# Hybrid attention and recurrence trunk: GpSimd's order waits taken out, its block products moved, and the recurrence's normalisation moved from ScalarE to VectorE

## The reference

```python
od = diff_attention(q, k, v, lam)         # 4 heads, two softmax maps each, block-causal mask of 64-token chunks
    # w = softmax(q1 k1) - lam * softmax(q2 k2);  out = w @ v
od = rms_norm(od, subln_g) * (1.0 - lam_init)
...
orr = hgrn2_chunked(qr, kr, vr, lf)       # 4 heads, state 128x128, k = 1 - f
    # S_t = diag(f_t) S_(t-1) + k_t v_t^T;  o_t = S_t^T q_t
orr = rms_norm(orr, hgrn_norm_g) * swish(gate)
x = x + concat(od, orr) @ w_out
x = x + SwiGLU(rms_norm(x))
```

## Time and profile before

| | |
|---|---|
| time, median of 3 runs | 2884.36 us (2879.38 to 2885.98) |
| time of the profiled execution | 2884.36 us |
| its span, first to last instruction | 2882.5 us |
| mean granted TensorE clock | 0.975 |
| busy: TensorE, its weight loads | 2706.1 us (94%), 2285.1 us (79%) |
| busy: VectorE, ScalarE, GpSimd | 1451.1 us (50%), 1084.1 us (38%), 224.8 us (8%) |

### The profile page before, as it was taken

The page is one execution under the profiler, slowest core; times in us unless marked ns, Lnnn a source line. Parts: engine busy times, 40 slices in busy tenths (PEclk is TensorE's granted clock), DMA queues, the critical chain, the costliest instruction groups (busy, mean ns, idle before and its releaser), DMA issues. The chain is left out here.

```text
span 2882.5 us, 33852 instructions
## 1 busy us (share of the span) xinstructions
PE 2706.1 (94%) x13648; PEld 2285.1 (79%) x13648; DVE 1451.1 (50%) x1920; ACT 1084.1 (38%) x1760; POOL 224.8 (8%) x186
## 2 busy tenths in 40 slices
PE   7999999995999999969968999998999997999999
PEld 6888888885888888857857888887888875888887
DVE  5434353423666666633446666667666654224221
ACT  4434343422576767662333222233222223113111
POOL 5000000003332324100000000000000000000000
PEclk9999999997999999979989999999999999999999
DMA  4545454447252523125853332243333216335332
GB/s 166 184 166 192 152 190 147 147 160 199 59 132 74 132 74 99 41 104 159 263 180 127 88 88 84 74 140 112 88 88 88 76 53 230 137 137 193 137 133 73
DMA packets 287578, 372.49 MB, mean 129 GB/s; under 512 B 15808, under 2 KB 175552, under 8 KB 285632
## 3 DMA queue, kind: packets, MB, share of 16 engines
q1 hardware_dynamic: 287424, 370.34, 40.6%
HBM read 265.43 MB, written 104.86 MB: 128 GB/s over the span
## 5 line engine op out<-in xcount | busy, mean ns | idle before, releaser
L1811 PE MATMUL gate_bank<-gate_b_hi,gate_a_hi 128*128 128x512 f32 x1232 | 482.8, 392 | 38.3 <-DVE first_b_lo L1690 20.5
L1813 PE MATMUL gate_bank<-gate_b_hi,gate_a_lo 128*128 128x512 f32 x1232 | 481.7, 391 | 0.0
L1812 PE MATMUL gate_bank<-gate_b_lo,gate_a_hi 128*128 128x512 f32 x1056 | 412.6, 391 | 0.0
L1811 PEld LDWEIGHTS gate_bank<-gate_b_hi,gate_a_hi 128*128 128x128 f32 x1232 | 233.0, 189 | 88.8 <-issue 21.7
L1994 PE MATMUL down_prod<-down_w_hi,down_f_hi 128*128 128x512 f32 x704 | 276.2, 392 | 19.0 <-DVE down_f_lo L1956 15.2
L1995 PE MATMUL down_prod<-down_w_lo,down_f_hi 128*128 128x512 f32 x704 | 274.9, 391 | 0.0
L1996 PE MATMUL down_prod<-down_w_hi,down_f_lo 128*128 128x512 f32 x704 | 274.7, 390 | 0.0
L1813 PEld LDWEIGHTS gate_bank<-gate_b_hi,gate_a_lo 128*128 128x128 f32 x1232 | 232.9, 189 | 48.6
L525 PE MATMUL proj_prod<-proj_w_hi,proj_h_hi 128*128 128x512 f32 x640 | 253.2, 396 | 6.8 <-DVE proj_w_lo L380 6.0
L1956 DVE TENSOR_TENSOR down_f_lo<-down_f_raw,down_f_hi 128x1408 fp32r<-128x1408 f32 x64 | 101.5, 1622 | 305.6 <-ACT down_f_hi L1929 305.2
L527 PE MATMUL proj_prod<-proj_w_hi,proj_h_lo 128*128 128x512 f32 x640 | 250.1, 391 | 0.0
(11 more groups left out here) (198 smaller groups left out, 4875.2 us busy)
## 6 DMA issues: line engine op xcount, KB each, us to landing
proj_w_raw<-in_w_in_dram SPq DMA_DIRECT2D x56, 1024.0 KB, 6.4
down_f_raw<-ff SPq DMA_DIRECT2D x64, 704.0 KB, 5.5
first_full<-in_w_gate_dram SPq DMA_DIRECT2D x88, 256.0 KB, 4.1
gate_full<-in_w_up_dram SPq DMA_DIRECT2D x88, 256.0 KB, 4.0
ff<-gate_c SPq DMA_DIRECT2D x66, 256.0 KB, 2.6
gate_b_lo<-operands SPq DMA_DIRECT2D x12, 1024.0 KB, 9.0
down_w_raw<-in_w_down_dram SPq DMA_DIRECT2D x22, 512.0 KB, 4.5
operands<-outp_made SPq DMA_DIRECT2D x40, 256.0 KB, 3.3
```

The lines of the kernel that those rows point to most:

```text
L1811: pe.matmul(dst, a_hi[:, pos, s, :], b_hi[pos][:, s, :], start=opens and s == 0, stop=False, skip_group_check=True)
L1812: pe.matmul(dst, a_hi[:, pos, s, :], b_lo[pos][:, s, :], start=False, stop=False, skip_group_check=True)
L1813: last = pe.matmul(dst, a_lo[:, pos, s, :], b_hi[pos][:, s, :], start=False, stop=s == HALF_SLABS - 1, skip_group_check=True)
```

## The change

It edits three engines of `mix_tokens`; nothing else of the kernel changes.

1. GpSimd: the wait `behind_combination` and the gate's wait for `combined` are gone. All seven products of block h are made at the start of block h, behind the gate of block h - 1, and not in two parts at the end of block h - 1.
2. ScalarE no longer scales `ro`. VectorE does, with one operation of 128x512 for each chunk (a broadcast of `ro_rrms` as its second input) in place of ScalarE's four of 128x128. In the running blocks VectorE does this at the end of the step before the chunk's, behind the reading of the second fill.
3. In the last block, ScalarE normalises the four attention chunks first and then copies all eight, while VectorE normalises the four recurrence chunks. The count for which the turns wait (`r_scaled`) changes with it.

```diff
--- before.py
+++ after.py
@@ -822,53 +822,29 @@
 
         @block.gpsimd
         def _(pool):
-            def product(h, m):
-                src = whole[m][:] if m else rf[:].rearrange("p h n -> p (h n)")
-                src = src.rearrange("p (n s) -> p n s", s=2)
-                if m:
-                    pool.wait_ge(whole_made, h * LEVELS + m)
-                nc.gpsimd.tensor_tensor(whole[m + 1][:], src[:, :, 0], src[:, :, 1], ALU.mult).then_inc(whole_made, 1)
-
-            def behind_combination(h, n):
-
-                step = h * STEPS + n // 2
-                if n % 2 == 0 and step:
-                    pool.wait_ge(combined, step)
-
-            def gate(h):
-                pool.wait_ge(rgate_in, 16 * (h + 1))
-                pool.wait_ge(fill_read, filled(h, len(FILLS) - 1))
-                if h + 1 < HEADS:
-                    pool.wait_ge(combined, (h + 1) * STEPS - 1)
-                nc.gpsimd.tensor_tensor(ro[:], ro[:], rgate[:], ALU.mult).then_inc(r_gated, 1)
-
             for h in range(HEADS):
-                if h == 0:
-                    pool.wait_ge(rf_in, 16)
-                    for m in range(LEVELS):
-                        product(h, m)
+                pool.wait_ge(rf_in, 16 * (h + 1))
+                for m in range(LEVELS):
+                    src = whole[m][:] if m else rf[:].rearrange("p h n -> p (h n)")
+                    src = src.rearrange("p (n s) -> p n s", s=2)
+                    if m:
+                        pool.wait_ge(whole_made, h * LEVELS + m)
+                    nc.gpsimd.tensor_tensor(whole[m + 1][:], src[:, :, 0], src[:, :, 1], ALU.mult).then_inc(whole_made, 1)
                 for side in range(2):
                     pool.wait_ge(fill_done, filled(h, fill_at("diagonal", side, HALF - 1)))
                     nc.gpsimd.tensor_tensor(half(rq, side), half(rq, side), half(rf, side), ALU.mult).then_inc(q_ready[side], 1)
                 for m in range(LEVELS):
                     for side in range(2):
-                        n = fill_at("level", side, m)
-                        pool.wait_ge(fill_done, filled(h, n))
-                        behind_combination(h, n)
+                        pool.wait_ge(fill_done, filled(h, fill_at("level", side, m)))
                         if m:
                             pool.wait_ge(k_ready[side], h * LEVELS + m)
                         nc.gpsimd.tensor_tensor(runs_of(rk, side, m, 0), runs_of(rk, side, m, 0), factor(side, m, 0), ALU.mult).then_inc(k_ready[side], 1)
                         pool.wait_ge(q_ready[side], h * UPDATES + m + 1)
                         nc.gpsimd.tensor_tensor(runs_of(rq, side, m, 1), runs_of(rq, side, m, 1), factor(side, m, 1), ALU.mult).then_inc(q_ready[side], 1)
-                if h + 1 < HEADS:
-                    pool.wait_ge(k_ready[1], (h + 1) * LEVELS)
-                    pool.wait_ge(q_ready[1], (h + 1) * UPDATES)
-                    pool.wait_ge(rf_in, 16 * (h + 2))
-                    for m in range(LEVELS - 1):
-                        product(h + 1, m)
-                    pool.wait_ge(fill_read, filled(h, len(FILLS) - 1))
-                    product(h + 1, LEVELS - 1)
-                gate(h)
+                pool.wait_ge(rgate_in, 16 * (h + 1))
+
+                pool.wait_ge(fill_read, filled(h, len(FILLS) - 1))
+                nc.gpsimd.tensor_tensor(ro[:], ro[:], rgate[:], ALU.mult).then_inc(r_gated, 1)
 
         @block.scalar
         def _(act):
@@ -927,19 +903,9 @@
                 nc.scalar.activation(o_rms[:], o_sumsq[:], ACT.Sqrt, bias=eps[:], scale=1.0 / P).then_inc(o_rms_made, 1)
 
             def normalise(h, c):
-
-                if c < TURNS:
-                    act.wait_ge(o_rrms_made, h + 1)
-                    for t in range(c * GROUP, (c + 1) * GROUP):
-                        nc.scalar.activation(o_all[h % 2][:, t, :], o_all[h % 2][:, t, :], ACT.Copy, scale=o_rrms[:, t:t + 1]).then_inc(o_normed, 1)
-                else:
-                    act.wait_ge(r_rrms_made, h + 1)
-                    act.wait_ge(r_gated, h + 1)
-                    head = c - TURNS
-                    for t in range(CH):
-                        part = ro[:, t, head * C:(head + 1) * C]
-                        at = t * HEADS + head
-                        nc.scalar.activation(part, part, ACT.Copy, scale=ro_rrms[:, at:at + 1]).then_inc(r_scaled, 1)
+                act.wait_ge(o_rrms_made, h + 1)
+                for t in range(c * GROUP, (c + 1) * GROUP):
+                    nc.scalar.activation(o_all[h % 2][:, t, :], o_all[h % 2][:, t, :], ACT.Copy, scale=o_rrms[:, t:t + 1]).then_inc(o_normed, 1)
 
             act.wait_ge(chain, 2)
             nc.scalar.activation(lam_exps[:], lam_dots[:], ACT.Exp).then_inc(lam_exp_made, 1)
@@ -966,13 +932,13 @@
                 if 0 < len(groups) <= 2:
                     read_output(s - 1)
                 if s == TOTAL + 1:
-                    normalise(HEADS - 1, 0)
+                    for c in range(TURNS):
+                        normalise(HEADS - 1, c)
                 for head, c in chunks_at(s):
-                    if s == TOTAL + 1 and c + 1 < CHUNKS:
-                        normalise(head, c + 1)
                     take_chunk(head, c)
                 for head, c in chunks_at(s + 1) if s < TOTAL else ():
-                    normalise(head, c)
+                    if c < TURNS:
+                        normalise(head, c)
 
         @block.vector
         def _(dve):
@@ -1035,6 +1001,16 @@
                 nc.vector.reciprocal(ro_rrms[:], ro_rms[:]).then_inc(r_rrms_made, 1)
                 dve.wait_ge(o_rms_made, h + 1)
                 nc.vector.reciprocal(o_rrms[:], o_rms[:]).then_inc(o_rrms_made, 1)
+
+            def normalise(h, c):
+
+                if c >= TURNS:
+                    dve.wait_ge(r_rrms_made, h + 1)
+                    dve.wait_ge(r_gated, h + 1)
+                    head = c - TURNS
+                    out = ro[:, :, head * C:(head + 1) * C]
+                    scale = ro_rrms[:].rearrange("p (c h) -> p c h", h=HEADS)[:, :, head]
+                    nc.vector.tensor_tensor(out, out, scale.unsqueeze(2).to_broadcast([P, CH, C]), ALU.mult).then_inc(r_scaled, 1)
 
             nc.vector.memset(state[:], 0.0)
             nc.vector.memset(early[:].bitcast(F32), 0.0).then_inc(masks_made, 1)
@@ -1068,6 +1044,8 @@
                     read_fill(h, 2 * j + 1)
                 if live and h and j == FIRST_CHUNK_STEP - 2 or s == TOTAL + 1:
                     invert_roots(h - 1)
+                for head, c in chunks_at(s + 1) if s <= TOTAL - 1 else chunks_at(s):
+                    normalise(head, c)
 
         @block.tensor
         def _(pe):
@@ -1118,7 +1096,7 @@
                 if c < TURNS:
                     pe.wait_ge(o_normed, h * STEPS + (c + 1) * GROUP)
                 else:
-                    pe.wait_ge(r_scaled, (h * HEADS + c - TURNS + 1) * CH)
+                    pe.wait_ge(r_scaled, h * HEADS + c - TURNS + 1)
                 open_slot(slot)
                 for t in range(GROUP):
                     src = o_all[h % 2][:, c * GROUP + t, :] if c < TURNS else ro[:, t, (c - TURNS) * C:(c - TURNS + 1) * C]
```

## The result

The changed kernel takes 2902.94 us (2901.63 to 2903.68, 4 runs) against 2883.95 (2879.38 to 2885.98, 4 runs): a ratio of 1.0066 [1.0053, 1.0081], 19.0 us slower. Its profiled execution took 2902.67 us, span 2901.0. The forecast was 2899.9 us. The first transfer of the next stage (L1289 before, L1267 after) starts at 1281.21 before and at 1299.55 after, so 18.3 us arose up to that point and 0.2 us behind it. The stage itself starts 0.5 us later after than before (first key load at 667.05 against 666.56). Totals are a coarser measure than this: the part behind that first transfer, which no edit of this document touches, took 1599.7 to 1605.0 us in the twelve profiles.

What follows compares the result with a forecast made beforehand. In narrow steps TensorE's own work plus every wait put before it was taken as the bound, in wide steps the score-maximum-exponential path. Terms 5.5 + 4.3 + 9.6 - 3.9 = +15.5 us on 2884.36 gave 2899.9 us, range 2885 to 2912.

Steps and rivals of the forecast that it cites:

- levels 5 and 6: In all four blocks GpSimd's multiplication gets ahead of the combination, making the turn 0.83 and 0.55 us late: 5.5 us.
- boundary: Between blocks, GpSimd's moved products hold the ratio and the combination of 1920 elements; 3 x 1.4 = 4.3 us slower.
- level 3: Late normalisations on VectorE let GpSimd's multiplications ahead of ratio and combination; turn 2.2 us late in three blocks.
- level 4: In step 6 a start some 0.3 us late lets GpSimd win here too: 1.0 us in each of three blocks.
- step 9: The collision of product and combination goes in three blocks; worth 0 to 0.5 us a block, taken as 0.
- tail: In the last block VectorE and ScalarE share the normalising, so the last copy ends 3.9 us earlier; bounds 3.5 and 4.2.
- GpSimd keeps its pairs together: Rival: both multiplications of a pair go ahead of the waiting combination; +27 us, 2912 us, chance 0.14.
- the tail alone: Rival: collisions fall into slack or VectorE wins them, so the gain of 3.9 us decides; 2880.5 us, chance 0.12.
- VectorE wins the close races: Rival: levels 5 and 6 cost nothing, the boundary 0.6 us, the normalisation only its lateness; 2886 us, chance 0.17.
- Start order decides: Rival: the earlier start takes the port shared by VectorE and GpSimd; +11.4 us, 2896 us, chance 0.12.

Runs made afterwards that it cites:

- a1_order: The kernel before with only the order wait taken out that held GpSimd's level multiplications behind the combination: 2890.67 us, ratio 1.0029.
- a2_products: The kernel before with only GpSimd's products moved behind the gate, which no longer waits for the combination: 2887.60 us, ratio 1.0020.
- b2_norm_order: The kernel before with the order wait gone and VectorE normalising the recurrence output in blocks 0 to 2; products and tail as before: 2904.45 us, ratio 1.0079.
- b3_stall: The kernel before with idle VectorE reductions ahead of the combination at step 5, four in blocks 0 and 3, nine in 1 and 2: 2898.12 us, ratio 1.0053.
- c0_before: The kernel before run and profiled once more, unchanged: 2883.96 us.
- b1_keep_order: The whole change, but with the wait kept that holds GpSimd's side 0 multiplications behind the step's combination: 2884.37 us, ratio 1.0005 against the kernel before.
- a4_tail: The kernel before with VectorE normalising the four recurrence chunks in the last block only, ScalarE the four attention chunks: 2881.21 us, ratio 0.9993.
- v3_four_stages: The kernel before with VectorE normalising all eight last-block chunks, four staging buffers for three, and products held past step 9's combination: 2873.06 us, ratio 0.9965.

## Why the prediction came out near, point by point

The forecast of +15.5 stands against 18.3 by the end of the stage, but the closeness flatters it: the two terms for the boundary and for what comes behind level 3 were 1.3 and 5.2 us too small, and a gain of 4.7 us that no term held, in good part luck, made up for most of that.

| term | predicted | measured in the stage | shown by |
|---|---|---|---|
| levels 5 and 6 | 5.5 | 5.7 | a1_order |
| boundary | 4.3 | 5.6 | a2_products |
| level 3 | 6.6 | 6.64 | b2_norm_order |
| after level 3 (level 4 in the prediction) | 3.0 | 8.15 | b2_norm_order, b3_stall |
| step 9 | none | −4.7 | c0_before, in part open |
| tail | −3.9 | −3.8 | b1_keep_order; −3.3 in a4_tail |
| first steps of the stage | none | +0.70 | open |

**Levels 5 and 6** went as written: GpSimd wins both, one multiplication each.

**The boundary.** The mechanism was right, only the size was off: "3 x 1.4 = 4.3 us" measured 1.87 each. The rule used was that the delay of the first turn passes on, forecast as 1.34 and measured as 1.45 us (822.32 against 820.26, less the 0.61 of lateness brought along). The combination of 1920 was 2.17 us late, not 2.05, and 0.56 of that came back by the next; another 0.26 was lost in the block's first step, which no term held; no run here shows by what.

**Level 3** turned round as written: the ratio held, the second multiplication ahead, 2.21, 2.22 and 2.21 us against 2.2. Here the rival that GpSimd keeps its pairs together is half right: its second multiplication goes first where it starts ahead of the combination (by 0.09 us), and not at levels 5 and 6, where the combination was already waiting and took its turn after one.

**Level 4 is the step that failed**: "enough for GpSimd to win level 4 too ... so 1.0 us". It did not win. The extra lateness of 0.3 us never came, since TensorE was late itself; the combination, 0.13 us ahead as the fills of before had put it, kept its length. The time up to the combination of 768 was lost all the same, and more of it: 3.25, 1.63 and 3.27 us. It lies on TensorE, whose granted clock falls to 0.50 after the wait of 2.1 us; matmuls of the next scores take 0.63 to 0.78 us, and the fill 2.96. b3_stall shows this with a stall of another origin. The prediction priced a wait on TensorE at its own length, and here that was 2.2 us of a bill of 3.8 to 5.5. It is also one of two reasons why order wait and normalisation don't add (21.8 us in the steps of b2_norm_order, against 7.9 for the two alone): the lower clock makes 9.5 us of it, and level 3's own stall of 2.2 us, in place of 0.58, needs both edits too.

**Step 9** was set to 0. Behind the 0.22 us regained from levels 5 and 6, the four blocks gave −1.48, −1.55, −0.11 and −1.55 in this pair of profiles. Where both profiles have the dip, or neither has it, the products' move is worth +0.06 us (a2_products, block 0) and −0.11 (block 2), so 0 was right for the combination itself. The rest is the dips that before has and the changed kernel's profile lacks. They come and go without any edit: c0_before lost one, and a4_tail, whose edit touches no step 9, lacks all three and has one in block 2, where before has none. Whether the products' move also makes them rarer isn't shown. The four profiles in which no product meets the combination of 1152 (changed kernel, a2_products, b1_keep_order, v3_four_stages) have 0, 2, 0 and 1 dips in four blocks, the other eight 1 to 4; that is too few to tell, and part of the −4.7 may belong to the change. A dip is 0.05% of the time, so profiles of two kernels must be compared step by step and not by their sums.

**The tail** was right by mechanism and size (a4_tail, with −3.3, lies just outside the bounds of 3.5 and 4.2). The limit that was named, the three staging buffers, is what v3_four_stages lifts: with four of them the tail falls from 22.10 to 20.80 us.

**Of the rivals**, the tail alone (−3.9) did decide nothing: the stalls came at every place priced. That VectorE wins the close races is excluded by levels 5 and 6. "Start order decides" falls too, by recorded starts: the combination lost when it started at the same time (737.79 against 737.79) and when it was 0.03 us ahead (819.18 against 819.21), and won when 0.13 ahead (878.44 against 878.57). The traces of all runs here agree: a combination that started up to 0.04 us ahead of a GpSimd operation was held by it, and one that started 0.13 us or more ahead was not. The Trainium skill, "SBUF — State Buffer", section "Who interferes with whom", says that issue order, not the shape of the operation, decides who blocks. With the lead of 0.13 us the trace agrees; with 0.03 the recorded start does not tell who was first, so that an order of issue which differs from it by some hundredths of a microsecond is not excluded.

**What stays open**: the lead between 0.03 and 0.13 us from which VectorE wins; what decides whether step 9 has a dip; why the clock stayed low for 3.4 us in block 2 and for 6.8 in blocks 1 and 3 of one execution, while b2_norm_order and b3_stall paid 3.1 to 3.3 us everywhere; and the 0.70 us by the first steps of block 0, of which 0.46 stand at the first combination already (two executions of before differ by 1.4 us there, so it may be chance).

## What to carry to other kernels

A wait that looks redundant can be what keeps two engines off one port: before taking one out, list for each pair of operations that share the port who starts how far ahead, since here a lead of 0.03 us lost and one of 0.13 kept the turn, with 0.8 us at stake. Price a new wait on TensorE not only at its length: one of 0.93 us cost 1.05 in all, one of 2.1 to 2.2 us cost 3.8 to 5.6, so two nearly harmless edits that land on the same step can cost more than their sum. Moving work off a loaded engine pays where that engine is alone on the path (the serial tail, 6.5 us), not where the receiving engine is (the narrow steps, which lost 2.2 us by it even with the order wait in place).

## What was not expected of the hardware

- The granted clock reacts to one wait: after a wait of 2.10 to 2.23 us a fill lasts 2.29 to 3.68 us in place of 2.00, and the clock is at 1.2 GHz, the lower of its two levels, for 3.4 to 6.8 us; after 0.93 us the fill keeps its 2.00 and the clock its 2.4 GHz.
- The same program gains or loses a dip at step 9, worth 1.4 us, from one execution to the next (PEclk 0.88 or 1.00 in the same 9 us).
- A waiting combination gets its turn after one multiplication (2.00 = 1.15 + 0.85), but a combination that starts while a second multiplication is already running waits for that one (866.09 against 866.18: 1.68 in place of 0.89).
- A one-element ratio behind a product of 1.90 us takes 1.50 us in place of 0.22.
- A normalisation of 512 elements takes 0.61 us alone, and a pair of them 2.70 beside one multiplication, which itself stretched from 1.16 to 1.61.
